# Attention's probabilities times values as two fp32r products with both parts of the values, and the stream's weights split in place

## The chip, the cores and the metric

The kernel runs on one core of one Trainium2 chip. The metric is device time in microseconds. Before the change the median of three runs is 1666.35 us (1666.28 to 1668.36).

## The reference, cut to what matters

One layer of a hybrid encoder, in fp32, over 1024 prompt frames and 64 new frames. D is 1024, there are 8 heads of 64 in each of two branches.

```python
z = rmsnorm(x, g_mix) @ w_in + b_in          # q,k,v of both branches, forget logits, two gates
# branch A: sliding window of 128, 8 q heads, 2 kv heads, bias and a sink per head
ya = softmax_with_sink(qa @ ka.T * SCALE + bias) @ va
# branch B: 8 heads, causal, logit += c[t] - c[s], c = cumsum(log_sigmoid(f))
yb = softmax(qb @ kb.T * SCALE + c_t - c_s) @ vb   # prompt: 1024 keys; new frames: 2048 cached + 64
x  = x + (sigmoid(ga) * (ya @ w_oa) + sigmoid(gb) * (yb @ w_ob)) @ w_out
x  = x + swiglu(rmsnorm(x))                   # then a final rmsnorm
```

The change touches `@ va` and `@ vb` of the prompt (and `@ va` of the new frames in branch A), and the order in which the weights of `w_in` are loaded and split.

## The kernel before, in words

Matmuls that must keep fp32's precision are made of fp32r matmuls (one pass each). An operand x is split into x_hi, a rounded copy that ScalarE writes as fp32r, and x_lo = x - x_hi, which VectorE writes. A product is then hi*hi + hi*lo + lo*hi, three matmuls (`split_product`, lines 2233 to 2235).

**Stages.** First x is normalised and transposed into `h_hi`, `h_lo`. Then the projection with `w_in` runs in 34 blocks of 128 output columns (`BLOCKS`). A block has three pieces (`dense(p)`, 24 matmuls each of 384, 384 and 320 columns), one for each third of the tokens. Pieces 0 to 17 stand before the stream. The **stream** is 136 attention units (steps 0 to 135) with pieces 18 to 85 laid between them, one in every even step. Units 0 to 71 are sliding-window units: four pairs of heads (`pair_start(p)` = 18p), nine tiles of 128 queries, two heads each. Units 72 to 135 are branch B's prompt ("fox"): four pairs, eight tiles, two heads; tile t has t + 1 blocks of 128 keys. Behind the stream stand four **decode units** (136 to 139, kind "new") for the 64 new frames with 2048 cached keys, with the last pieces 86 to 101 between them. Then come the merge with `w_oa`, `w_ob` and `w_out`, and the feed-forward part, which the change leaves as it is.

**A step.** Every engine has a list of instructions of its own in program order, and semaphores between them. TensorE's step n is `turn(n)` (transposes of unit n's probabilities into PSUM banks 4 and 5, four blocks to a group; line 2308), `scores(n + 2)` (line 2291), the transposes of `turns_at[n]`, `dense(piece_at(n))` if n is even, and `outputs(n - 1)` (line 2331): for each block of keys one matmul with the transposed probabilities as weights and 64 columns of values moving, plain fp32. In odd steps `turns_at` holds ("ot", n - 2), the transpose of the finished output of two units (line 2343); it waits for `o_evac`, the normalisation of unit n - 2. In even steps it holds ("tok", ...), keys and values turned to token order.

ScalarE's step n is `exp(n + 1)` (lines 1081 and 1083), `evac(piece_at(n - 1))` (line 1070, and behind a block's third piece `split_hi` of the block two further, line 1038), the even groups of `empty_groups` (line 561: PSUM to `probT` in SBUF), then the high parts of what was turned and staged. VectorE's step n is the odd groups of `empty_groups`, `scores(n + 2)` (line 1531: bias added, maximum taken), the low parts, `split_lo` (line 1478: `w_lo` = `w_raw` - `w_hi`), and `normalise(n - 1)` (lines 1553, 1554, 1562: the row sum's reciprocal, then bank 6 scaled into `o_tok`). With `outputs(n)` TensorE waits for the groups of unit n (`emptied`), and for `o_evac` of unit n - 1.

**Weights.** `w_raw`, `w_hi` and `w_lo` have two slots each. SyncE's queue loads block n once the low part of block n - 2 is written (`load_chunk`, lines 574 to 579), so loads run far ahead of their use. In the decode units `load_block(32)` stands before the first unit and `load_block(33 + s)` at the end of SyncE's part for unit s; `load_cache(s + 2)`, which loads the next cached keys into `kc_raw`, stands before it and waits until TensorE has turned all of the previous ones. TensorE's part of decode unit s is turn, cache part 0, piece d = 87 + 4s, cache part 1, outputs, cache part 2, piece d + 1, cache part 3, piece d + 2, output turn ("ots", line 2361), scores of the next unit, piece d + 3. The output turn waits for everything turned earlier to be emptied (`misc_done`).

```python
load_new(s + 1); load_values(s + 1)        # SyncE, decode unit s, before
...
if s < 2:
    load_cache(s + 2)
if s < 3:
    load_block(33 + s)
```

## Time and profile before

| | |
|---|---|
| median of the runs | 1666.35 us |
| the profiled execution | 1668.92 us, span 1667.1 us |
| TensorE matmul busy | 1609.9 us, 97% |
| TensorE weight loads | 1510.1 us, 91% |
| VectorE busy | 1018.6 us, 61% |
| ScalarE busy | 665.8 us, 40% |
| chain that ended last | TensorE 89%, DMA 4%, VectorE 4% |
| granted clock, mean | 0.989 |

The profiled execution is one run of the program; what lies around its span (1.8 us) is start and end. Matmuls are pipelined: the duration of one (some 275 ns) is longer than the time from its start to the next one's start, and only the latter adds up. So lists of rows in order of time are read by their starts. The stream lies from about 126 to 619 us, the decode units from there to 744 us.

### The profile page before, as it was taken

How to read it: one execution, taken by the hardware profiler on the slowest of the kernel's cores; microseconds unless marked ns; L12 is line 12 of the kernel's file. 1: busy time of each engine (PE TensorE's matmuls, PEld its weight loads, DVE VectorE, ACT ScalarE, POOL GpSimd, SP SyncE). 2: the span in 40 equal slices, each digit the busy share in tenths (PEclk: the TensorE clock that was granted, in tenths of full speed). 3: DMA queues.
4: the chain of work that ended last, by engine and by line, in shares of the span. 5: the costliest groups of instructions: out<-in, count | busy, mean ns of one | idle time of the engine just before them, and what ended most of it. 6: DMA issues, size and time to landing. Idle time of an engine off the chain costs nothing.

```text
span 1667.1 us, 27671 instructions
## 1 busy us (share of the span) xinstructions
PE 1609.9 (97%) x10556; PEld 1510.1 (91%) x10556; DVE 1018.6 (61%) x2232; ACT 665.8 (40%) x1333; POOL 174.7 (10%) x312
## 2 busy tenths in 40 slices
PE   6999999999999998999999899999999999989997
PEld 5999999999999998987898799999999999878886
DVE  6546556555546454426366586776677777659865
ACT  5335445544445434334253462222222223424443
POOL 3011111000000001012011000000122222110000
PEclk8999999999999999999999999999999999999999
DMA  6044331553351425648555323332344445766532
GB/s 205 26 127 131 121 107 66 181 163 95 116 146 47 120 91 166 193 148 283 187 158 198 120 76 104 98 97 78 100 154 154 154 154 180 245 188 188 152 121 94
DMA packets 190290, 230.59 MB, mean 138 GB/s; under 512 B 14807, under 2 KB 140280, under 8 KB 189640
## 3 DMA queue, kind: packets, MB, share of 16 engines
q1 hardware_dynamic: 163616, 138.71, 28.4%
q0 software_dynamic: 26544, 90.12, 15.3%
q8 instruction: 85, 1.39, 0.4%
q14 instruction: 45, 0.37, 0.1%
HBM read 166.76 MB, written 62.08 MB: 137 GB/s over the span
## 4 chain that ended last, share of the span: by engine, by line
PE 89%; DMA 4%; DVE 4%; issue 2%; ACT 1%; SPq 0%; POOL 0%; DVEq 0%; POOLq 0%
PE ps L2233 23%; PE ps L2235 23%; PE ps L2234 23%; PE ps L2331 6%; PE ps L2291 4%; PE ps L2308 3%; PE ps L2343 1%; PE ps L2511 1%; PE ps L2510 1%; DMA w_raw<-in_w_ob_dram 1%; DMA w_raw<-in_w_out_dram 1%; DMA xa<-in_x_prompt_dram 1%; PE ps L2254 1%; ACT w_hi L1038 1%; PE ps L2350 0%
## 5 line engine op out<-in xcount | busy, mean ns | idle before, releaser
L2233 PE MATMUL ps<-h_hi,w_hi 128*128 128x384 f32 (+1 forms) x816 | 275.1, 337 | 1.8 <-DVE w_lo L1478 1.1
L2235 PE MATMUL ps<-h_hi,w_lo 128*128 128x384 f32 (+1 forms) x816 | 268.2, 329 | 0.0
L2234 PE MATMUL ps<-h_lo,w_hi 128*128 128x384 f32 (+1 forms) x816 | 268.2, 329 | 0.0
L2235 PE MATMUL ps<-t_hi,e_lo 128*128 128x272 f32 x704 | 203.5, 289 | 0.0
L2234 PE MATMUL ps<-t_lo,e_hi 128*128 128x272 f32 x704 | 202.9, 288 | 0.0
L2233 PE MATMUL ps<-t_hi,e_hi 128*128 128x272 f32 x704 | 201.5, 286 | 0.9 <-DVE silu L1898 0.9
L2233 PE MATMUL ps<-b_hi,e_hi 128*128 128x272 f32 x528 | 152.4, 289 | 6.4 <-ACT p L1355 5.1
L2233 PEld LDWEIGHTS ps<-h_hi,w_hi 128*128 128x128 f32 x816 | 155.2, 190 | 3.2 <-DVE w_lo L1478 1.4
L2234 PEld LDWEIGHTS ps<-h_lo,w_hi 128*128 128x128 f32 x816 | 155.2, 190 | 0.5 <-issue 0.5
L2235 PEld LDWEIGHTS ps<-h_hi,w_lo 128*128 128x128 f32 x816 | 154.8, 190 | 0.0
L1562 DVE TENSOR_SCALAR o_tok<-ps,rinv 128x64 f32<-128x64 f32 x136 | 38.6, 283 | 188.9 <-PE ps L2331 186.7
L2235 PE MATMUL ps<-b_hi,e_lo 128*128 128x272 f32 x528 | 153.3, 290 | 0.0
L2234 PE MATMUL ps<-b_lo,e_hi 128*128 128x272 f32 x528 | 153.0, 290 | 0.0
L2233 PEld LDWEIGHTS ps<-t_hi,e_hi 128*128 128x128 f32 x704 | 132.8, 189 | 1.1 <-issue 1.1
L2235 PEld LDWEIGHTS ps<-t_hi,e_lo 128*128 128x128 f32 x704 | 132.4, 188 | 0.0
L2234 PEld LDWEIGHTS ps<-t_lo,e_hi 128*128 128x128 f32 x704 | 132.2, 188 | 0.0
L1070 ACT ACTIVATE stg<-ps,bin_cols 128x384 f32<-128x384 f32 (+1 forms) x96 | 53.8, 562 | 183.7 <-PE ps L2235 183.6
L2233 PE MATMUL ps<-e_hi,f_hi 128*128 128x512 f32 x308 | 120.9, 393 | 5.2 <-DVE e_lo L2116 5.2
L1083 ACT ACTIVATE sprob<-sprob,negm 128x256 f32<-128x256 f32 (+8 forms) x140 | 92.3, 659 | 77.0 <-DVE negm L1537 76.5
L2235 PE MATMUL ps<-e_hi,f_lo 128*128 128x512 f32 x308 | 120.8, 392 | 0.0
L2234 PE MATMUL ps<-e_lo,f_hi 128*128 128x512 f32 x308 | 120.8, 392 | 0.0
L1478 DVE TENSOR_TENSOR w_lo<-w_raw,w_hi 128x1024 fp32r<-128x1024 f32 x66 | 80.6, 1221 | 65.0 <-ACT w_hi L1038 64.7
(338 smaller groups left out, 3607.0 us busy)
## 6 DMA issues: line engine op xcount, KB each, us to landing
w_raw<-in_w_gu_dram SPq DMA_DIRECT2D x104, 256.0 KB, 3.3
w_raw<-in_w_in_dram SPq DMA_DIRECT2D x68, 256.0 KB, 3.2
zg_d<-stg POOLq DMA_DIRECT2D x28, 544.0 KB, 3.1
act_d<-act POOLq DMA_DIRECT2D x44, 272.0 KB, 2.7
s_d<-s_sum POOLq DMA_DIRECT2D x44, 256.0 KB, 3.3
f_raw<-s_d SPq DMA_DIRECT2D x44, 256.0 KB, 2.9
f_raw<-act_d SPq DMA_DIRECT2D x33, 256.0 KB, 3.0
w_raw<-in_w_out_dram SPq DMA_DIRECT2D x32, 256.0 KB, 3.4
```

The lines of the kernel that those rows point to most:

```text
L1038: nc.scalar.copy(w_hi[:, slot, :], w_raw[:, slot, :]).then_inc(w_hi_done, 1)
L1070: nc.scalar.activation(out, ps[:, bank_of(p), 0:c1 - c0], ACT.Identity, bias=bin_cols[:, col:col + 1]) \
L1083: nc.scalar.activation(probs, probs, ACT.Exp, bias=negm[0:R, c], accum_out=rowsum[0:R, c]).then_inc(p_ready, 1)
L1478: nc.vector.tensor_tensor(w_lo[:, slot, :], w_raw[:, slot, :], w_hi[:, slot, :].bitcast(F32), ALU.subtract) \
L1562: ins = nc.vector.tensor_scalar(o_tok[0:R, tl, HD * e:HD * e + HD], ps[0:R, 6, 0:HD], rinv[0:R, c], None, ALU.mult)
L2233: nc.tensor.matmul(out, l_hi, r_hi, start=start, stop=False)
L2234: nc.tensor.matmul(out, l_hi, r_lo, start=False, stop=False)
L2235: return nc.tensor.matmul(out, l_lo, r_hi, start=False, stop=stop)
L2254: last = nc.tensor.transpose(ps[:, norm_bank(tag, t, q), P * k:P * k + R], src[:, P * (4 * q + k):P * (4 * q + k) + P], ident[0:R, 0:R])
L2291: last = nc.tensor.matmul(ps[0:R, 2 + pc % 2, 0:w], lhsT, rhs, start=k == 0, stop=k == last_k and "diagonal" not in piece)
L2308: last = nc.tensor.transpose(ps[0:K, 4 + g % 2, (blk - b0) * R:(blk - b0) * R + R], score_room(u)[:, P * blk:P * blk + K], ident[0:R, 0:R])
L2331: last = nc.tensor.matmul(ps[0:R, 6, 0:w], probT[0:K, p0:p0 + R], val, start=blk == 0, stop=blk == nb - 1)
```

## The change

For stream units the transposed probabilities are split into `probT_hi` (in `probT`'s place) and `probT_lo` (in `w_lo`'s place), and the values into `va_parts` and `vb_parts`, which hold high and low parts side by side, 128 columns. For each block TensorE issues two fp32r matmuls of 128 columns, one with `probT_hi` and one with `probT_lo` as weights. Bank 6 then holds two halves whose sum is the output; `normalise` scales one and adds the other scaled. ScalarE writes the high part of every group, VectorE the low part. The decode units keep the fp32 product.

As `w_lo` is taken, blocks 6 to 29 (`IN_PLACE`) write their low part over `w_raw` (`w_rest`). A slot is then free only when TensorE has done its block, so the loads wait for `z_pe`. Splits of blocks 8 to 31 move: in the stream to four steps behind the last piece of block n - 2, in the decode units to the places below. Several tiles of the attention get other addresses, with the waits that follow from them.

```diff
+IN_PLACE = range(6, 30)
...
             def load_chunk(n, slot, parts):
-                if not isinstance(n, int) or n >= 2:
+                if n - 2 in IN_PLACE:
+                    sp.wait_ge(z_pe, 3 * (n - 1))
+                    hold()
+                elif n >= 2:
                     sp.wait_ge(w_lo_done, n - 1)
...
+            def load_pair_values(p):
+                if p > 4:
+                    sp.wait_ge(sem("s_k_lo"), value_count["b", p - 1, 1])
+                sp.dma_start(vb_tok[:, :, :, :], pv_fox[:, :, P * (p - 4):P * (p - 4) + P].rearrange("q t (e c) -> q t e c", e=2)) \
+                    .then_inc(sem("v_landed"), 16)
...
-                if step >= 1 and piece_at(step - 2) is not None and piece_at(step - 2) % 3 == 2:
-                    load_block(piece_at(step - 2) // 3 + 4)
+                d = piece_at(step - 1) if step else None
+                if d is not None and d % 3 == 2:
+                    load_block(d // 3 + 2)
...
-            load_block(32)
+            load_block(30)
             for s in range(4):
                 if s < 3:
                     load_new(s + 1)
...
                 if s < 2:
                     load_cache(s + 2)
-                if s < 3:
-                    load_block(33 + s)
+                if s == 0:
+                    load_block(31)
+                elif s < 3:
+                    load_block(30 + 2 * s)
+                    load_block(31 + 2 * s)
...
             pool.wait_ge(o_ready, N_UNITS)
-            pool.dma_start(gffn_row[:, :], g_ffn.broadcast_to([P, D])).then_inc(sem("gffn_landed"), 16)
             for j in range(5, KD):
                 load_gates(0, j)
             for slot in range(2):
                 pool.wait_ge(sem(f"abs_saved{slot}"), 64 * 2)
+            pool.dma_start(gffn_row[:, :], g_ffn.broadcast_to([P, D])).then_inc(sem("gffn_landed"), 16)
...
-                if s == 2:
+                if s == 2 and not 8 <= n + 2 < 32:
                     split_hi(n + 2, n % 2)
+
+            def values_hi(what):
...
+                if kind == "b":
+                    a.wait_ge(sem("v_landed"), 16 * (n - 3))
+                    a.wait_ge(o_ready, pair_start(n))
...
+                nc.scalar.copy(hi, raw).then_inc(sem("s_k_hi"), 1)
+
+            def turned_groups_hi(n):
+
+                u = units[n]
+                if n >= 2:
+                    a.wait_ge(o_ready, n - 1)
+                for g in range(u["group0"], u["group1"]):
+                    a.wait_ge(pt_ready, g + 1)
+                    for rows, cols, src in group_views(u, g):
+                        ins = nc.scalar.copy(probT_hi[rows, cols], src)
+                    ins.then_inc(sem("pt_act"), 1)
...
-                empty_groups(a, nc.scalar.copy, 0, units[n])
+                for what in values_at.get(n, ()):
+                    values_hi(what)
+                turned_groups_hi(n)
...
+            def turned_groups_lo(n):
+
+                u = units[n]
+                for g in range(u["group0"], u["group1"]):
+                    v.wait_ge(sem("pt_act"), g + 1)
+                    for rows, cols, src in group_views(u, g):
+                        ins = nc.vector.tensor_tensor(probT_lo[rows, cols], src, probT_hi[rows, cols].bitcast(F32), ALU.subtract)
+                    ins.then_inc(sem("pt_dve"), 1)
...
-                    ins = nc.vector.tensor_scalar(o_tok[0:R, tl, HD * e:HD * e + HD], ps[0:R, 6, 0:HD], rinv[0:R, c], None,
-                                                  ALU.mult)
+                    out = o_tok[0:R, tl, HD * e:HD * e + HD]
+                    chained(nc.vector.tensor_scalar(out, ps[0:R, 6, HD:P], rinv[0:R, c], None, ALU.mult))
+                    ins = nc.vector.scalar_tensor_tensor(out=out, in0=ps[0:R, 6, 0:HD], scalar=rinv[0:R, c], in1=out, op0=ALU.mult,
+                                                         op1=ALU.add)
...
+                    if u["kind"] == "new":
+                        last = nc.tensor.matmul(ps[0:R, 6, 0:P], probT[0:K, p0:p0 + R], val, start=blk == 0, stop=blk == nb - 1)
+                    else:
+                        nc.tensor.matmul(ps[0:R, 6, 0:P], probT_hi[0:K, p0:p0 + R], val, start=blk == 0, stop=False)
+                        last = nc.tensor.matmul(ps[0:R, 6, 0:P], probT_lo[0:K, p0:p0 + R], val, start=False, stop=blk == nb - 1)
```

In the decode units ScalarE's `split_hi(30)` now stands behind the second evacuation of unit 0, before the last cache part, and `split_hi(31)` behind the first evacuation of unit 1; `split_hi(32)` stays where it was, behind the second evacuation of unit 1 (piece 92). VectorE's low parts follow them. `values_at` puts the values' splits at steps 34 and `pair_start(p)` + 1 and + 2; those of the first two pairs stand before step 0.

## Rows read from the trace of the kernel before

**Rows 1.** Busy time by stage: stretch, its length, then busy (xcount) per engine, clock, DMA
```profile
126.00:344.00 218.00, 215.37 (x1452) 204.77 (x1451) 128.43 (x528) 107.48 (x332) 28.06 (x45) 1.00 0.37 118
344.00:619.00 275.00, 274.08 (x1975) 267.71 (x1976) 147.07 (x513) 130.98 (x280) 14.53 (x27) 1.00 0.39 116
```

**Rows 2.** The instructions of line 2331: duration min/median/max, first and last start
```profile
L2331 PE MATMUL ps<-vb_tok,probT x576: 217/275/295, 356.2 to 619.1; 128*128 128x64 f32 x192
...
L2331 PE MATMUL ps<-va_tok,probT x272: 217/275/323, 126.1 to 355.2; 128*128 128x64 f32 x120, 128*64 128x64 f32 x8, 64*64 64x64 f32 x8
```

**Rows 3.** In order of time: start, duration, engine, line, count; six fp32 products
```profile
602.79 1.45 PE L2331 MATMUL ps<-vb_tok,probT 128*128 128x64 f32 x12
...
604.08 0.93 PE L2308 MATMUL ps<-ident,sprob 128*128 128x128 f32 x7
```

**Rows 4.** In order of time: fp32r matmuls of 128 columns in a row
```profile
437.13 0.22 PE L2291 MATMUL ps<-k_stack,q_hi 128*128 128x128 f32 x1
...
437.19 0.27 PE L2291 MATMUL ps<-k_stack,q_lo 128*128 128x128 f32 x1
...
437.30 0.28 PE L2295 MATMUL ps<-causal_r,ident_r 128*128 128x128 f32 x1
```

**Rows 5.** In order of time: an odd sliding-window step around the output turn
```profile
203.00 0.28 DVE L1562 TENSOR_SCALAR o_tok<-ps,rinv 128x64 f32<-128x64 f32 x1 [1.01 <-PE ps L2331]
...
203.40 0.14 PEld L2343 LDWEIGHTS ps<-ident,o_tok 128*128 128x128 f32 x1 [0.26 <-issue]
...
203.56 0.48 DVE L1531 CUSTOM_DVE_ANT_0 sprob<-ps,bias,sink_rows 128x256 f32<-128x256 f32 x1
...
204.53 0.16 DVE L1554 RECIPROCAL rinv<-rowsum 128x1 f32<-128x1 f32 x1
...
204.73 0.28 DVE L1562 TENSOR_SCALAR o_tok<-ps,rinv 128x64 f32<-128x64 f32 x1
204.87 0.18 ACT L1083 ACTIVATION_READ_ACCUMULATOR sprob<-sprob,negm 128x1 f32 x1
```

**Rows 6.** Waits of TensorE's weight loads, 126 to 620 us: total, times, longest
```profile
PEld ps L2343 <- issue: 8.5, 33, 0.3
```

**Rows 7.** Groups of instructions of VectorE and ScalarE, 126 to 619 us: busy, mean ns
```profile
L561 DVE COPY probT<-ps 128x256 f32<-128x256 f32 x40 | 17.0, 424 | 1.9 <-PE ps L2308 1.8 <-issue 0.2
...
L1586 DVE TENSOR_TENSOR ot_lo<-ps,ot_hi 128x128 fp32r<-128x128 f32 x63 | 18.0, 285 | 0.0
...
L1478 DVE TENSOR_TENSOR w_lo<-w_raw,w_hi 128x1024 fp32r<-128x1024 f32 x22 | 26.8, 1218 | 0.1
...
L561 ACT COPY probT<-ps 128x256 f32<-128x256 f32 x32 | 11.3, 352 | 0.0
...
L1038 ACT CAST w_hi<-w_raw 128x1024 fp32r<-128x1024 f32 x22 | 22.8, 1036 | 0.0
```

**Rows 8.** In order of time: TensorE's waits around decode unit 0
```profile
630.46 0.66 PE L2308 MATMUL ps<-ident,sprob 128*128 128x128 f32 x4 [1.22 <-ACT probT L561]
...
654.11 0.50 PE L2291 MATMUL ps<-ks,qs_hi 128*128 128x512 f32 x1 [1.58 <-DVE maxpart L1531]
```

**Rows 9.** In order of time: the last cache part of decode unit 1
```profile
677.91 0.37 SPq L646 DMA_DIRECT2D kc_raw<-in_cache_fox_k_dram  x1
...
678.84 1.18 ACT L1100 CAST ks<-ps 64x512 fp32r<-64x512 f32 x2
...
680.24 1.39 DVE L1511 TENSOR_TENSOR ks<-ps,ks 64x512 fp32r<-64x512 f32 x2
...
681.92 0.27 PE L2361 MATMUL ps<-ident,o_tok 128*64 128x128 f32 x1
```

**Rows 10.** DMA issues: count, KB each, us to landing; 677 to 690, then 600 to 745
```profile
kc_raw<-in_cache_fox_k_dram SPq DMA_DIRECT2D x1, 1024.0 KB, 7.5
...
w_raw<-in_w_in_dram SPq DMA_DIRECT2D x4, 256.0 KB, 4.0
```

**Rows 11.** Busy time and granted clock, columns as in rows 1
```profile
956.00:960.00 4.00, 2.45 (x11) 2.48 (x12) 2.50 (x4) 2.87 (x6) 0.00 (x0) 0.50 0.04 13
```

More of the change, by code:

```diff
@@ L465, in build_program @@
                     pieces[-1]["diagonal"] = (P * t % 512, P, causal_r[:, :])
-                    units.append(dict(kind="fox", pair=p, rows=P, v=[vb_tok[s][:, j, HD * e:HD * e + HD] for j in range(t + 1)],
+                    units.append(dict(kind="fox", pair=p, rows=P, v=[vb_parts[:, j, e, :] for j in range(t + 1)],
                                       e=e, t=t, first=LOWEST, pieces=pieces))
@@ L495, in emptied, with value_views @@
         def emptied(g):
-            return sem(("pt_act", "pt_dve")[g % 2]), g // 2 + 1
+            if g < stream_groups:
+                return sem("pt_dve"), g + 1
+            return sem(("pt_act", "pt_dve")[g % 2]), stream_groups + (g - stream_groups) // 2 + 1
+        values = [("a", kv, x) for kv in range(2) for x in range(2)] + [("b", p, x) for p in range(4, 8) for x in range(2)]
+        value_count = {what: 7 + k for k, what in enumerate(values)}
+        values_at = {34: [("a", 1, 0), ("a", 1, 1)]}
+        for p in range(4, 8):
+            for x in range(2):
+                values_at[pair_start(p) + 1 + x] = [("b", p, x)]
+        def value_views(what):
+            kind, n, x = what
+            if kind == "a":
+                rows, tiles = (slice(0, P), slice(0, NT)) if x == 0 else (slice(0, DEC), slice(NT, NT + 1))
+                parts = va_parts[n]
+                return va_tok[rows, tiles, HD * n:HD * n + HD], parts[rows, tiles, 0:HD], parts[rows, tiles, HD:P]
+            tiles = slice(0, 2) if x == 0 else slice(2, NPT)
+            return vb_tok[:, tiles, :, :], vb_parts[:, tiles, :, 0:HD], vb_parts[:, tiles, :, HD:P]
         turns_at = {step: [] for step in range(N_STREAM)}
@@ L1191, in _ @@
                     stage_hi(what)
+                d = piece_at(n - 4) if n >= 4 else None
+                if d is not None and d % 3 == 2:
+                    split_hi(d // 3 + 2, d // 3 % 2)
             exp(N_STREAM)
@@ L1197, in _ @@
                 d = 87 + 4 * s
-                empty_groups(a, nc.scalar.copy, 0, units[N_STREAM + s])
+                empty_new(a, nc.scalar.copy, 0, units[N_STREAM + s])
                 if s < 3:
@@ L1477, in split_lo, with values_lo @@
                 v.wait_ge(w_hi_done, n + 1)
-                nc.vector.tensor_tensor(w_lo[:, slot, :], w_raw[:, slot, :], w_hi[:, slot, :].bitcast(F32), ALU.subtract) \
+                rest = w_rest if n in IN_PLACE else w_lo
+                nc.vector.tensor_tensor(rest[:, slot, :], w_raw[:, slot, :], w_hi[:, slot, :].bitcast(F32), ALU.subtract) \
                     .then_inc(w_lo_done, 1)
+            def values_lo(what):
+                raw, hi, lo = value_views(what)
+                v.wait_ge(sem("s_k_hi"), value_count[what])
+                nc.vector.tensor_tensor(lo, raw, hi.bitcast(F32), ALU.subtract).then_inc(sem("s_k_lo"), 1)
+            def turned_groups_lo(n):
+                u = units[n]
+                for g in range(u["group0"], u["group1"]):
+                    v.wait_ge(sem("pt_act"), g + 1)
+                    for rows, cols, src in group_views(u, g):
+                        ins = nc.vector.tensor_tensor(probT_lo[rows, cols], src, probT_hi[rows, cols].bitcast(F32), ALU.subtract)
+                    ins.then_inc(sem("pt_dve"), 1)
             def norm_recip_a(R, t):
@@ L1716, in _ @@
             scores(1)
+            values_lo(("a", 0, 0))
+            values_lo(("a", 0, 1))
             for n in range(N_STREAM):
-                empty_groups(v, nc.vector.tensor_copy, 1, units[n])
+                turned_groups_lo(n)
+                for what in values_at.get(n, ()):
+                    values_lo(what)
                 if n + 2 < N_STREAM:
@@ L2330, in outputs @@
                     p0 = turned_at(u) + blk * R
-                    last = nc.tensor.matmul(ps[0:R, 6, 0:w], probT[0:K, p0:p0 + R], val, start=blk == 0, stop=blk == nb - 1)
+                    if u["kind"] == "new":
+                        last = nc.tensor.matmul(ps[0:R, 6, 0:P], probT[0:K, p0:p0 + R], val, start=blk == 0, stop=blk == nb - 1)
+                    else:
+                        nc.tensor.matmul(ps[0:R, 6, 0:P], probT_hi[0:K, p0:p0 + R], val, start=blk == 0, stop=False)
+                        last = nc.tensor.matmul(ps[0:R, 6, 0:P], probT_lo[0:K, p0:p0 + R], val, start=False, stop=blk == nb - 1)
                 last.then_inc(o_ready, 1)
```

151 lines of the change are left out of this document (89 added, 62 removed).

## The prediction

> **What bounds the kernel now.** I read the busy time by stage first, then the waits, then stretches in order of time. In the stream (126 to 619 us) TensorE is busy for 215.37 of 218 and 274.08 of 275 us at full granted clock, while VectorE has 128 and 147 us of work and ScalarE 107 and 131 [rows 1]. So a step of the stream ends when TensorE's own list of instructions ends. Two kinds of edit can move the time there: one that changes what TensorE issues, or one that makes it wait. After the stream, in the four decode units, waits on VectorE and ScalarE do reach TensorE [rows 8].
>
> **The products.** The 424 products of probabilities and values stand as 848 matmul records, 576 and 272 [rows 2]: an fp32 product runs as two matmuls, each with its own weight load. Twelve records, six products, take 604.08 - 602.79 = 1.29 us, so one product costs 0.215 us [rows 3]. The new form issues two fp32r matmuls of 128 columns, each with its own weight load: again 848 records. What one costs shows where fp32r products of 128 columns stand in a row: when its weights had been waiting, the next came 0.06 us later (437.13 to 437.19), and with a load to make 0.11 us later (437.19 to 437.30) [rows 4]. The new kernel changes weights at every matmul, so I take the 0.11: two cost 0.22, against 0.215. The 64 idle columns that the old form leaves are given away free of charge, but nothing is won, because the weight load already sets the pace. 424 x 0.005 = 2 us; records after a wide matmul are hidden, so I take **+1** (ends: -41, below, and +2).
>
> The Trainium skill, page "TensorE: Matmul & The Clock Gate", section "Weight-path perf modes", says that the fast weight load is on for 128 weights unless the input is FP32. If fp32r counted as "not FP32", the change would win. Its section on LDWEIGHTS prices an ordinary load at columns over 1.2 per ns, 107 ns for 128, an estimate that would make two products 0.21 us; the 0.11 us in rows 4 agrees with that slow load.
>
> **Emptying the transposed probabilities.** Before, ScalarE and VectorE empty alternate groups. Now ScalarE copies every group as high part (256 columns: 352 ns) and VectorE then subtracts every group; a subtraction of 128 columns takes 285 ns and a VectorE copy of 256 takes 424 [rows 7], so I price a subtraction like a copy. It is a chain now: high part, low part, VectorE's scores, exp, next high part, which ScalarE's order puts after that exp. Scores and exp run from 203.56 to 205.05, 1.5 us [rows 5]; with 0.05 for each handover a sliding-window step is 0.35 + 0.42 + 1.5 + 0.1 = 2.4 us, a pair of steps 4.8, plus about 0.6 for the evacuation of the dense piece: 5.4. TensorE's pair is 218 / 36 = 6.1 us [rows 1]. The dense piece in every second step covers the chain, so this costs **0** while the chain is shorter. VectorE's load rises by 36 x 0.42 + 72 x 0.32 = 38 us in the sliding-window stage, to about 170 of 230, and by about as much in the fox stage. For the steps where token copies, split queries and values add to one another's delay I take **+2** (ends 0 and 20).
>
> **The extra operation in the normalisation.** The two halves of the output must be added: a scale, a wait on itself, and a scaled add, 0.28 + 0.04 + 0.28 where 0.28 stood (0.04 lies between the reciprocal's end at 204.69 and 204.73) [rows 5], +0.32 us. Who waits: in odd steps TensorE turns the output pair (L2343) right after scoring, and needs that normalisation. It ends at 203.28 and the weight load of the turn goes at 203.40, after a gap of 0.26 us [rows 5]. The waits list 33 such gaps, 8.5 us [rows 6]: none of these has cover left. By the loops, four of them open the fox pairs, where the value split below hides them, and 29 lie in the sliding-window stage: 29 x 0.32 = **+9.3**. In the fox pairs wider scores cover it from the fourth tile on; some twelve steps have less cover than 0.32 and no gap so far, I take 0.15 each, **+1.8** (0 to 3.8). The last output of the stream has none: **+0.3**.
>
> **Values split in the stream.** At each fox pair's start outputs wait for the first two value tiles to be split. That waits until the previous pair's last output is done, then 0.35 on ScalarE, the high part of a 128-wide group (about 0.25), its low part 0.29, the values' low part 0.42, and 0.2 of handovers: 1.6 us. TensorE has 0.9 of other work and waiting. 4 x 0.75 = **+3.0** (0 to 6). The remaining tiles have three steps of cover; those of the sliding window are split in VectorE's idle time before step 0 and beside a dense piece.
>
> **Weights split in place.** The low part overwrites the raw weights, so block n can be loaded only when the dense pieces of block n-2 are done, on SyncE's queue; it has six steps, some 20 us, before its first piece, and its split is due four steps after the release. Loads take 4 to 7.5 us to land [rows 10]. load_pair and load_new stand before some blocks on SyncE, but their waits are met a step or more earlier. No cost in the stream.
>
> Behind the stream the order changes. In decode unit 0, block 30 is no longer split before the turned groups, so the 1.22 us wait goes [rows 8], and block 31's split no longer stands before the scores, so the 1.58 us goes [rows 8]. But block 30's split (1.0 on ScalarE, 1.2 on VectorE) [rows 7] now stands before the last cache part, for which TensorE's output turn waits, so I let 1.1 us come back. Sum **-1.7** (-2.8 to 0).
>
> In decode unit 1 the new order hurts. Block 32 is now loaded behind load_cache(3), which waits for TensorE's fourth cache turn, so it is issued after kc_raw at 677.91, at 678.3. ScalarE splits block 32 right after its second evacuation (which had cost it nothing, as the load had long landed) and stands in order: behind it are the high parts of the cache (678.84) and of the new keys. VectorE's low part (680.24 to 681.63) waits for them, and TensorE's output turn (681.92) and the scores behind it wait for all [rows 9]. kc_raw took 7.5 us to land, block loads of the decode stage 4.0 in the median [rows 10]; sharing the queue with kc_raw, I take 7.5. Then: landed 686.0; high part of the block 687.1; cache high 688.3; block low 688.35; cache low 689.75; output turn 0.3 later, 690.05. The dense piece before it ends at 681.9 and covers nothing beyond that. **+8.1** (4.5 with 4.0 us). This is also 8 us of silence for TensorE: from 956 to 960 us, where TensorE stood and then resumed (busy 2.45 of 4), the granted clock was 0.50, the lower of the two levels (1.2 GHz) [rows 11]; 2 us of work then take 4. **+2** (0 to 4). Blocks 34 and 35 come later too; 34 now goes where 35 went, a dense piece and the next unit's scores ahead of its split: 0.
>
> The gffn load moves down GpSimd's queue, ahead of the second token group's loads, whose product it precedes by a whole output projection: 0.
>
> **Sum.** 1 + 2 + 9.3 + 1.8 + 0.3 + 3.0 - 1.7 + 8.1 + 2 = 25.8 us. The profiled execution took 1668.92 (span 1667.1, 1.8 around it), which gives 1694.7; it is 2.6 above the median of the runs, 1666.35, so on the median the forecast is 1692.
>
> **Rivals.** (a) Fast loads, the faster side: the fp32r weight load does not set the pace and a product of 128 columns costs the 0.06 of rows 4. Then 424 x (0.215 - 0.12) = 41 us go on TensorE, and with all else as above the time is 1666 + 26 - 1 - 41 = 1650. Against it: the 0.11 of rows 4 is just this load. (It is the skill's fast-load rule above, read that way.) Chance 0.08. (b) The chain bounds: if handovers and queued extras make the chain of two sliding-window steps 6.8 us instead of 5.4, it passes TensorE's 6.1 + 0.3, and 0.4 x 36 pairs = 14 us, and as much again in the fox pairs, come on top: 1720. It decides from 1.0 us more per pair than I count. For it: VectorE's token copies and splits stand in the same queue. Against: VectorE stays below three quarters busy. Chance 0.13. (c) Less than I say: block 32 lands in 4 us and the clock stays up (-5.6), value waits are covered (-3.0), collisions don't occur (-2): 1681. Chance 0.15. (d) No change: the output gap and the wait in unit 1 both hidden, 1668; against it every one of the 33 gaps. Chance 0.04. The forecast, 1683 to 1705: 0.60.
>
> The likeliest is 1692; the range 1676 to 1712 takes in (c) and the near half of (b). About 0.2% is what a measurement of this kernel can tell from no change: faster 0.08, same 0.04, slower 0.88.
>
> **What would show it.** L2331's successor: spacing 0.11 with two fp32r records per product (0.06 would prove rival a). The gap before the output turn about 0.55 instead of 0.26. One wait of 7 to 8 us before TensorE's output turn in decode unit 1, with ScalarE waiting for w_raw's DMA, and a dip of the granted clock behind it; no 1.58 us wait in unit 0. If TensorE's busy share in the stream drops below 0.95 at many small waits on probT or negm, rival (b) holds. I am wrong altogether if the stream is shorter than 493 us.

## The result and the profile after

The kernel after takes 1691.8 us (median; 1691.5 to 1693.4), the kernel before 1667.2 in the runs beside it (1666.3 to 1668.4): ratio 1.0147, 95% interval 1.0132 to 1.0161, so 24.6 us slower. The profiled execution of after has a span of 1689.7 us, 22.6 more than before's.

Busy time by stage (stretch, length, then busy us and count of TensorE, its weight loads, VectorE, ScalarE and GpSimd, granted clock, DMA); the stream now ends at 636 us, so the second row is longer than that of [rows 1]:

```profile
126.00:344.00 218.00, 205.73 (x1378) 195.74 (x1377) 153.47 (x601) 113.92 (x351) 28.06 (x45) 1.00 0.35 111
344.00:640.00 296.00, 290.45 (x2046) 281.11 (x2046) 202.36 (x671) 157.88 (x355) 14.52 (x27) 0.99 0.36 108
640.00:767.00 127.00, 112.44 (x697) 102.83 (x697) 46.65 (x103) 42.47 (x72) 10.16 (x19) 0.95 0.56 169
```

In the same 218 us TensorE is busy 205.73 us where it was busy 215.37 [rows 1]. Its products still make 848 records in the stream; it waits. Where, the waits of its weight loads say (total, times, longest; first 126 to 344 us, then, in the second block, 344 to 640):

```profile
PEld ps L2462 <- issue: 17.2, 31, 0.9
PEld ps L2462 <- DVE o_tok L1668: 0.5, 1, 0.5
```

```profile
PEld ps L2462 <- issue: 6.0, 16, 0.6
PEld ps L2449 <- DVE probT_lo L1582: 1.9, 4, 0.6
```

L2462 is the turn of an output pair (L2343 before). `issue` is idle time for which this view names no releaser; for such a gap TensorE's matmul rows name the normalisation, as in the last line of the next list. In [rows 6] the turn had 33 gaps of 8.5 us in the whole stream, 0.26 each; the 31 gaps of the first block are 0.55 each, the size that the prediction gave as its sign. L2449 is the product with the high part of the probabilities; its four waits are the four fox pair starts. In order of time, the products and an odd sliding-window step of after:

```profile
196.74 0.22 PE L2449 MATMUL ps<-va_parts,probT_hi 128*128 128x128 f32 x1
196.80 0.28 PE L2450 MATMUL ps<-va_parts,probT_lo 128*128 128x128 f32 x1
196.91 0.27 PE L2449 MATMUL ps<-va_parts,probT_hi 128*128 128x128 f32 x1
197.02 0.28 PE L2450 MATMUL ps<-va_parts,probT_lo 128*128 128x128 f32 x1
197.13 0.41 PE L2423 MATMUL ps<-ident,sprob 128*128 128x128 f32 x2
...
197.41 0.28 DVE L1667 TENSOR_SCALAR o_tok<-ps,rinv 128x64 f32<-128x64 f32 x1 [1.95 <-PE ps L2450]
197.73 0.28 DVE L1668 SCALAR_TENSOR_TENSOR o_tok<-ps,rinv,o_tok 128x64 f32<-128x64 f32 x1
...
198.16 0.30 PE L2462 MATMUL ps<-ident,o_tok 128*128 128x128 f32 x1 [0.38 <-DVE o_tok L1668]
```

The records stand 0.06 us apart behind the wide dense matmul and 0.11 apart from then on, as forecast. The two operations of the normalisation follow each other 0.32 us apart, and the turn waits for the second.

The decode stage has the wait that was forecast in unit 1. First its loads on SyncE's queue, then ScalarE's wait for the second of them, VectorE behind it, TensorE's output turn (L2480) behind that, in order of time:

```profile
694.08 0.37 SPq L692 DMA_DIRECT2D kc_raw<-in_cache_fox_k_dram  x1
694.56 6.00 SPq L619 DMA_DIRECT2D w_raw<-in_w_in_dram  x4
...
703.10 1.04 ACT L1089 CAST w_hi<-w_raw 128x1024 fp32r<-128x1024 f32 x1 [8.93 <-DMA w_raw<-in_w_in_dram]
704.05 1.17 ACT L1177 CAST ks<-ps 64x512 fp32r<-64x512 f32 x2
...
705.43 1.39 DVE L1615 TENSOR_TENSOR ks<-ps,ks 64x512 fp32r<-64x512 f32 x2
...
706.88 0.13 PEld L2480 LDWEIGHTS ps<-ident,o_tok 128*64 128x64 f32 x1 [8.95 <-DVE ks L1615]
```

The same stretch by its granted clock (length, TensorE busy, clock, DMA share, GB/s), which goes to half, the lower of its two levels:

```profile
698.00:702.00 4.00, 0.25 (x2) 0.84 1.08 359
702.00:706.00 4.00, 0.00 (x0) 0.50 0.58 175
706.00:710.00 4.00, 2.77 (x7) 0.50 0.03 8
710.00:714.00 4.00, 3.99 (x19) 0.88 0.04 8
```

To see where time goes in several kernels I took from each trace the starts of TensorE's output turns. They divide the execution at the same instructions everywhere (us from the start of the span to the first of them, then between these starts: the sliding-window stage from its first output turn to its last, the fox stage from there to the last output turn of the stream, then decode units 0 to 3 each to its own turn, then the rest of the span):

| kernel | to first turn | sliding window | fox | unit 0 | unit 1 | unit 2 | unit 3 | rest |
|---|---|---|---|---|---|---|---|---|
| before | 131.7 | 224.2 | 272.2 | 22.2 | 31.7 | 30.3 | 31.4 | 923.5 |
| after | 130.0 | 235.9 | 280.2 | 21.2 | 39.6 | 31.7 | 31.2 | 919.9 |
| e1_w32_early | 131.9 | 236.1 | 281.8 | 21.2 | 30.8 | 30.3 | 29.8 | 921.7 |
| e2_one_scale | 128.8 | 231.6 | 276.1 | 21.2 | 39.4 | 32.5 | 31.7 | 921.3 |
| e3_before_two_scales | 129.2 | 234.2 | 278.4 | 23.7 | 31.7 | 30.3 | 29.8 | 921.8 |
| e4_low_twice | 129.8 | 247.3 | 306.0 | 21.2 | 40.0 | 31.5 | 31.1 | 920.7 |
| e5_64_columns | 131.7 | 230.8 | 276.9 | 21.2 | 39.6 | 32.1 | 31.6 | 921.0 |
| e6_high_only | 129.5 | 227.9 | 253.6 | 21.2 | 39.5 | 31.8 | 31.3 | 921.1 |
| e7_before_new_order | 131.2 | 224.2 | 272.1 | 21.6 | 30.2 | 30.3 | 30.9 | 922.3 |
| e8_turn_low_first | 129.3 | 222.2 | 276.1 | 21.2 | 39.7 | 31.7 | 31.4 | 920.9 |
| e9_both_orders | 131.9 | 223.1 | 272.1 | 21.6 | 30.2 | 30.3 | 31.1 | 922.9 |
| e10_change_reordered | 130.2 | 234.0 | 279.0 | 21.2 | 30.8 | 30.3 | 31.4 | 920.3 |

The table settles where: 11.7 us in the sliding-window stage, 8.0 in the fox stage, 8.0 in unit 1 and 1.3 behind it, less 1.7 ahead of the stream, 1.0 in unit 0, 0.2 in unit 3 and 3.6 behind the decode stage. To the rounding that is the 22.6 us between the two spans.

### The profile page after: what moved, and what is told of

It reads as the page before. It is cut to its first block, busy times and chain, and to the rows that moved or that the text cites. A ratio compares the mean times of both kernels' runs of the same rounds, so it can differ in the third digit from the quotient of the medians.

```text
span 1689.7 us, 27986 instructions
## 1 busy us (share of the span) xinstructions
PE 1616.1 (96%) x10556; PEld 1513.5 (90%) x10556; DVE 1100.1 (65%) x2468; ACT 701.0 (41%) x1433; POOL 174.6 (10%) x312
## 4 chain that ended last, share of the span: by engine, by line
PE 89%; DVE 5%; DMA 2%; issue 2%; ACT 1%; SPq 1%; POOL 0%; DVEq 0%; ACTq 0%; POOLq 0%
PE ps L2348 24%; PE ps L2350 24%; PE ps L2349 24%; PE ps L2406 4%; PE ps L2450 3%; PE ps L2449 3%; PE ps L2423 3%; PE ps L2447 1%; PE ps L2462 1%; DVE o_tok L1667 1%; PE ps L2630 1%; PE ps L2629 1%; DVE o_tok L1668 1%; DMA xa<-in_x_prompt_dram 1%; PE ps L2469 1%
## 5 line engine op out<-in xcount | busy, mean ns | idle before, releaser
L2350 PE MATMUL ps<-h_hi,w_rest 128*128 128x384 f32 (+1 forms) x576 | 187.8, 326 | 0.0
L1667 DVE TENSOR_SCALAR o_tok<-ps,rinv 128x64 f32<-128x64 f32 x136 | 38.6, 284 | 119.2 <-PE ps L2450 116.7
L1423 ACT CAST e_hi<-w_sum 128x512 fp32r<-128x512 f32 x88 | 54.1, 616 | 134.3 <-DVE w_sum L1982 105.9
L2350 PEld LDWEIGHTS ps<-h_hi,w_rest 128*128 128x128 f32 x576 | 108.1, 188 | 0.0
```

The lines of the kernel that those rows point to most:

```text
L1423: nc.scalar.copy(e_hi[:, q % RING, :], src).then_inc(sem("e_hi_done"), 1)
L1667: chained(nc.vector.tensor_scalar(out, ps[0:R, 6, HD:P], rinv[0:R, c], None, ALU.mult))
L2350: return nc.tensor.matmul(out, l_lo, r_hi, start=False, stop=stop)
```

## The experiments

**The late load.** e1_w32_early:

```
-                elif s < 3:
-                    load_block(30 + 2 * s)
-                    load_block(31 + 2 * s)
+                    load_block(32)
+                elif s == 1:
+                    load_block(33)
+                elif s == 2:
+                    load_block(34)
+                    load_block(35)
```

> The kernel after, with one load moved on SyncE's queue: block 32 is issued in decode unit 0, behind block 31, in place of unit 1 behind the third cache part. My theory: the long wait before TensorE's output turn in unit 1 (9.0 us on VectorE's ks in the trace of after, with ScalarE 8.9 us on w_raw's DMA) comes from that load alone, and so does the granted clock of 0.50 behind it; both go: 8.8 + 1.1 = 10 us less than after, about 1682 (1680 to 1684). Rival: the order of the splits on ScalarE and VectorE in unit 1 is what costs, and the wait only changes its name: 1690 to 1692, with a wait of several us on another instruction in the same place.

It took 1684.1 us, ratio 1.0111 (1.0092 to 1.0131), that is 18.7 over before in the runs beside it (1665.3; the kernels of this section ran on several chips, so each is compared with before on its own). In its trace the four decode units take 112.2 us, 11.6 less than after (123.7): 8.8 in unit 1 and 1.3 and 1.4 in the two behind it. The 1.4 in unit 3 are not the load's. There the granted clock is 0.58 from 752 to 756 us in after, 0.57 from 726 to 730 us in before, and 1.00 throughout in e1 and in e3 below, which has the old loads; e10 below has e1's loads, shows 0.65 there and takes 31.4 us for the unit again. The load is worth 8.8 + 1.3 = 10.1 us. The loads go ahead of unit 1, and ScalarE splits the block with no wait behind its evacuation:

```profile
670.72 2.20 SPq L619 DMA_DIRECT2D w_raw<-in_w_in_dram  x4
...
688.79 0.58 ACT L1124 ACTIVATE stg<-ps,bin_cols 128x384 f32<-128x384 f32 x1 [3.02 <-PE ps L2353]
689.27 1.03 ACT L1092 CAST w_hi<-w_raw 128x1024 fp32r<-128x1024 f32 x1
```

The clock stays up (columns as above):

```profile
702.00:706.00 4.00, 3.62 (x15) 1.00 1.07 356
```

So the load alone makes that wait; the rival falls. The whole execution gained only 5.9 us against before, since outside the decode units this profile was 5.5 us longer than after's with the same instructions: at the start (a stretch at clock 0.57, 108 to 112 us, where after had 1.00), at the end of the stream (0.66 and 0.50 from 636 to 644 us, where after had 0.59 and 1.00) and in the rest. Its four runs spread from 1680.5 to 1686.2.

**The second operation, taken from after and put into before.** e2_one_scale (in after) and e3_before_two_scales (in before):

```
-                    chained(nc.vector.tensor_scalar(out, ps[0:R, 6, HD:P], rinv[0:R, c], None, ALU.mult))
-                    ins = nc.vector.scalar_tensor_tensor(out=out, in0=ps[0:R, 6, 0:HD], scalar=rinv[0:R, c], in1=out, op0=ALU.mult,
-                                                         op1=ALU.add)
+                    ins = nc.vector.tensor_scalar(out, ps[0:R, 6, 0:HD], rinv[0:R, c], None, ALU.mult)
```

```
-                    ins = nc.vector.tensor_scalar(o_tok[0:R, tl, HD * e:HD * e + HD], ps[0:R, 6, 0:HD], rinv[0:R, c], None,
-                                                  ALU.mult)
+                    out = o_tok[0:R, tl, HD * e:HD * e + HD]
+                    chained(nc.vector.tensor_scalar(out, ps[0:R, 6, 0:HD], rinv[0:R, c], None, ALU.mult))
+                    ins = nc.vector.scalar_tensor_tensor(out=out, in0=ps[0:R, 6, 0:HD], scalar=rinv[0:R, c], in1=out, op0=ALU.mult,
+                                                         op1=ALU.max)
```

> The kernel after with the old single operation in the normalisation: it scales the first 64 columns of the product only, so the low parts of the values are left out of the result; the products themselves, the splits and the loads stay. My theory: the second operation and its wait on itself lie on TensorE's path in the 29 odd steps of the sliding-window stage without cover (29 x 0.38 = 11), in some of the fox steps (1.8) and at the last output (0.3): 13 us less than after, 1679 (1676 to 1681). Rival: what lengthened the steps is the chain high part, low part, scores, exp; then the operation gives back 3 us at most, 1689 or more.

> The kernel before with a second, dependent operation in the normalisation and nothing else: a scale, a wait on itself, then a scaled maximum with the result (which leaves every value as it was). My theory: the same +13 us as in the other direction (11 to 16), so 1680 against 1667. Rival: in the old kernel the gaps before the output turn were made by something other than the end of the normalisation and there is cover: +4 at most, 1671.

e3 took 1681.2, ratio 1.0090 (1.0071 to 1.0108), 15.8 us more than before: 10.0 in the sliding-window stage, 6.2 in the fox stage. e2 took 1684.0, ratio 1.0112 (1.0096 to 1.0129), only some 6 us less than after, counted from before on each chip, where I had said 13. By stage it gives back 4.3 and 4.1, while its decode units take 1.0 longer. Put in, the operation costs 10.0 us in the sliding-window stage; taken out, it gives 4.3 back, and 7.4 us remain that are not its. That spoke for something like the rival. The waits of TensorE's weight loads from 126 to 344 us show what (L2460 in e2 is the output turn, L2467 and L2469 are the turns of a token block, which use the same room, bank 7; in e3, the first block, the output turn is L2345):

```profile
PEld ps L2345 <- issue: 17.7, 32, 0.7
```

```profile
PEld ps L2460 <- issue: 7.0, 29, 0.3
PEld ps L2467 <- DVE ot_lo L1690: 5.7, 14, 0.5
PEld ps L2469 <- DVE ot_lo L1690: 3.5, 8, 0.6
```

With one operation the gaps ahead of the output turn are back at their old size (29 of 7.0 us; before has 30 of 7.7 in this stretch), and 22 waits of 9.2 us are new: the token turn waits until VectorE has made the low part of the output turn (ot_lo). Both kernels in the same step, before first, then e2:

```profile
209.47 0.28 DVE L1562 TENSOR_SCALAR o_tok<-ps,rinv 128x64 f32<-128x64 f32 x1 [3.40 <-PE ps L2331]
209.69 0.42 DVE L561 COPY probT<-ps 128x256 f32<-128x256 f32 x1
210.03 0.48 DVE L1531 CUSTOM_DVE_ANT_0 sprob<-ps,bias,sink_rows 128x256 f32<-128x256 f32 x1
...
210.62 0.28 DVE L1586 TENSOR_TENSOR ot_lo<-ps,ot_hi 128x128 fp32r<-128x128 f32 x1
```

```profile
210.64 0.28 DVE L1667 TENSOR_SCALAR o_tok<-ps,rinv 128x64 f32<-128x64 f32 x1 [1.52 <-PE ps L2448]
211.27 0.42 DVE L1582 TENSOR_TENSOR probT_lo<-ps,probT_hi 128x256 fp32r<-128x256 f32 x1 [0.35 <-ACT probT_hi L1149]
211.61 0.48 DVE L1635 CUSTOM_DVE_ANT_0 sprob<-ps,bias,sink_rows 128x256 f32<-128x256 f32 x1
...
212.20 0.28 DVE L1690 TENSOR_TENSOR ot_lo<-ps,ot_hi 128x128 fp32r<-128x128 f32 x1
```

In before VectorE copied the turned group itself, 0.22 us after the start of its scale. Now it must wait for ScalarE's high part. That starts at 210.87, 0.23 us after the start of the scale, about where the copy stood: the evacuation ahead of it on ScalarE (0.58 us) has just ended. It takes 0.37 us, and only then the low part can begin. So the low part starts 0.63 us after the start of the scale, 0.41 later than the copy did, and everything behind it on VectorE, scores and ot_lo, shifts by as much. The kernel after, in the same step, has this too, but there VectorE fills its 0.35 us of waiting with the second operation, and the low part again starts 0.63 us after the start of the scale:

```profile
211.52 0.28 DVE L1667 TENSOR_SCALAR o_tok<-ps,rinv 128x64 f32<-128x64 f32 x1 [1.50 <-PE ps L2450]
211.84 0.28 DVE L1668 SCALAR_TENSOR_TENSOR o_tok<-ps,rinv,o_tok 128x64 f32<-128x64 f32 x1
212.15 0.42 DVE L1582 TENSOR_TENSOR probT_lo<-ps,probT_hi 128x256 fp32r<-128x256 f32 x1
...
213.08 0.28 DVE L1692 TENSOR_TENSOR ot_lo<-ps,ot_hi 128x128 fp32r<-128x128 f32 x1
```

So the two causes hide in each other. From one output turn to the next there are 24 pairs of steps with a token turn and, behind them, 11 without; against before they are longer, in sum (us, from the same starts as the table above):

| kernel | 24 pairs with token turn | 11 pairs without |
|---|---|---|
| e3_before_two_scales (second operation alone) | +6.5 | +3.5 |
| e2_one_scale (high and low parts alone) | +7.8 | -0.3 |
| after (both) | +8.1 | +3.6 |
| e8_turn_low_first (e2 without the path, below) | -1.6 | -0.4 |

One such pair, behind step 27, takes 6.16 us in before, 6.58 in e2 and 6.57 in after; one without, behind step 57, 5.67, 5.69 and 6.02.

**The path through ot_lo.** Taken out of e2's form by e8_turn_low_first:

```
+                early = [ev for ev in turns_at[n] if ev[0] == "ot"] if n < 70 else []
+                for ev in early:
+                    turned_lo(ev)
                 if n + 2 < N_STREAM:
                     scores(n + 2)
                 for ev in turns_at[n]:
-                    turned_lo(ev)
+                    if ev not in early:
+                        turned_lo(ev)
```

> e2_one_scale, with VectorE making the low part of the output turn ahead of its scores in the sliding-window stage, in place of behind them; nothing else. My theory: the 7.4 us that e2_one_scale still has over before in the sliding-window stage (231.6 against 224.2 from its first output turn to its last) are token turns that wait for this low part; the 22 waits on ot_lo (9.2 us) go and the stage is back at 224 to 226: 5.5 to 7.5 us less than e2_one_scale, 1677 to 1679. Rival: scores now come 0.3 us later and their exponentials and transposes with them, so the wait moves to TensorE's transposes of the probabilities: 1683 to 1685.

1675.2 us, ratio 1.0061 (1.0044 to 1.0078). The sliding-window stage takes 222.2 us, 9.4 less than e2's and 2.0 less than before's; no wait on ot_lo is left in it, and the output turn has its old gaps (the same view, same stretch):

```profile
PEld ps L2464 <- issue: 7.3, 30, 0.3
PEld ps L2464 <- DVE o_tok L1667: 0.2, 1, 0.2
```

The path is shown. It gave more than I expected of it, and the scores 0.3 us later cost nothing.

**Is the chain of high and low parts near the limit?** e4_low_twice:

```
+                        chained(nc.vector.tensor_tensor(probT_lo[rows, cols], src, probT_hi[rows, cols].bitcast(F32), ALU.subtract))
                         ins = nc.vector.tensor_tensor(probT_lo[rows, cols], src, probT_hi[rows, cols].bitcast(F32), ALU.subtract)
```

> The kernel after with the subtraction that makes the low part of the turned probabilities done twice, the second behind a wait on the first: the chain from high part to the output products is 0.33 to 0.73 us longer for each group, and VectorE has 72 x 0.46 = 33 us more to do in the sliding-window stage and about 64 x 0.8 = 51 in the fox pairs. My theory: TensorE's own list sets the time in the stream and the dense piece of every second step covers the chain, so it costs little: +0 to +3 in the sliding-window stage, +0 to +8 in the fox pairs (VectorE would be at 0.86 of that stage), 1692 to 1703. Rival (the chain of ScalarE and VectorE bounds the steps): half of the 84 us or more comes through, 1734 or above.

1730.4 us, ratio 1.0394 (1.0378 to 1.0411). That is 38.6 more than after's 1691.8, and 40.4 more when each is counted from before on its own chip. My theory of that moment failed: nearly half of the added 84 us comes through, as the rival said. In the sliding-window stage it is 11.4 us: 10.9 in the 24 pairs with a token turn, where 24 x 0.46 (0.42 and the wait on itself) would make 11.0, and 0.5 in the 11 without. That fits the ot_lo path again, not a limit of the chain as such. In the fox pairs it is 25.8 us, where TensorE's weight loads now wait for VectorE in many steps (344 to 640 us):

```profile
PEld ps L2407 <- DVE maxpart L1636: 6.2, 18, 0.5
PEld ps L2424 <- issue: 4.4, 7, 1.3
PEld ps L2424 <- DVE probT_lo L1583: 4.1, 9, 0.9
```

So in the fox pairs the low part was covered once, and not twice.

**What sets the pace of a product.** e5_64_columns makes both products of e2_one_scale 64 columns wide:

```
-                        nc.tensor.matmul(ps[0:R, 6, 0:P], probT_hi[0:K, p0:p0 + R], val, start=blk == 0, stop=False)
-                        last = nc.tensor.matmul(ps[0:R, 6, 0:P], probT_lo[0:K, p0:p0 + R], val, start=False, stop=blk == nb - 1)
+                        nc.tensor.matmul(ps[0:R, 6, 0:HD], probT_hi[0:K, p0:p0 + R], val[:, 0:HD], start=blk == 0, stop=False)
+                        last = nc.tensor.matmul(ps[0:R, 6, 0:HD], probT_lo[0:K, p0:p0 + R], val[:, 0:HD], start=False, stop=blk == nb - 1)
```

e6_high_only leaves the product with probT_lo out of after:

```
-                        nc.tensor.matmul(ps[0:R, 6, 0:P], probT_hi[0:K, p0:p0 + R], val, start=blk == 0, stop=False)
-                        last = nc.tensor.matmul(ps[0:R, 6, 0:P], probT_lo[0:K, p0:p0 + R], val, start=False, stop=blk == nb - 1)
+                        last = nc.tensor.matmul(ps[0:R, 6, 0:P], probT_hi[0:K, p0:p0 + R], val, start=blk == 0, stop=blk == nb - 1)
```

> e2_one_scale with both output products 64 columns wide in place of 128: the low parts of the values leave the products too (they were already left out of the result). My theory: the weight load of 0.11 us sets the pace of these products, whatever their columns, so the time is that of e2_one_scale, 1684 (1682 to 1686), and the records stand 0.11 us apart as before. Rival (the columns set the pace, 64 of them for each of 848 records, some 0.027 us each at the spacing of wide matmuls in the trace): up to 20 us less, 1664 to 1675.

> The kernel after without the product of the low parts of the probabilities (their subtraction on VectorE stays, its result is not used): 424 matmul records fewer, 144 in the sliding-window stage and 280 in the fox pairs, of 0.11 us each. Plain sum if TensorE's list alone set the time: 15.8 + 30.8 = 47 us less, 1645. My theory now, from e2_one_scale: in the 24 pairs of steps that have a token turn, that turn waits for the low part of the output turn, which VectorE makes behind the low part of the probabilities and its scores; that path does not get shorter, so these pairs give back nothing (at most 0.1 us each), and the sliding-window stage shrinks by 12 x 0.44 = 5 to 8 us of the 15.8; the fox pairs give most of their 31. Sum 34 to 39 less, 1653 to 1658.

e5 took 1686.4, ratio 1.0128 (1.0111 to 1.0144), against e2's 1.0112: the intervals overlap, and of the rival's up to 20 us nothing came. Its products, in order of time:

```profile
198.68 0.27 PE L2448 MATMUL ps<-va_parts,probT_lo 128*128 128x64 f32 x1
198.79 0.28 PE L2447 MATMUL ps<-va_parts,probT_hi 128*128 128x64 f32 x1
198.91 0.28 PE L2448 MATMUL ps<-va_parts,probT_lo 128*128 128x64 f32 x1
```

Half the columns, the same 0.11 us. The weight load sets the pace, and the rival of the columns falls. (The new kernel, too, has 0.06 us between two records only where the weights had been waiting behind a wide matmul.) e6 took 1658.7, ratio 0.9957 (0.9943 to 0.9972), 33 us less than after and not the 47 of the plain sum: 8.0 of 15.0 in the sliding-window stage and 26.6 of 31.7 in the fox stage. (The expectation counts 144 and 280 records; by the trace they are 136 and 288, at 0.11 us each.) The 24 pairs with token turns gave 4.3 of their 10.1, the 11 without 3.7 of 4.6. I had said 34 to 39; the fox stage gave 5 less than all. In it weight loads now wait for VectorE's maxima (2.6 us in 8 waits between 338 and 600 us), about half of that.

**Putting the orders right.** e10_change_reordered is the whole change with e1's loads, e8's order, and in VectorE's stream loop values_lo ahead of turned_groups_lo:

```
+                for what in values_at.get(n, ()):
+                    values_lo(what)
                 turned_groups_lo(n)
-                for what in values_at.get(n, ()):
-                    values_lo(what)
```

> The whole change with three orders mended: block 32's load early (e1_w32_early), the output turn's low part ahead of the scores in the sliding-window stage (e8_turn_low_first), and the values' low part ahead of the turned probabilities' low part on VectorE. My theory, by stage: decode units 112.2 us as in e1_w32_early in place of 123.7 (-11.5); the sliding-window stage is then left with the second operation of the normalisation alone, 232 to 234 in place of 235.9 (-2 to -4, less than the sum of both causes, since each hides in the other); the four pair starts -0.3 to -0.4 each (-1.5). Sum -15 to -17: 1675 to 1677 (a little more where the clock dips as it did in e1_w32_early), still 8 to 11 slower than before. Rival: the two causes in the sliding-window stage add up, and it goes to 228 or below.

1678.4 us, ratio 1.0072 (1.0055 to 1.0089), 11.5 over before, where I had said 8 to 11. The sliding-window stage is at 234.0, where e3, the old kernel with the second operation alone, is at 234.2: that operation is all that is left of the change there. The causes did not add up; taking the smaller one away gave 1.9 us, not 9.4. The four pair starts gave 0.4, 0.2, 0.3 and 0.3. The decode units take 113.7, 1.5 more than I said, and that is the clock in unit 3 (0.65 from 740 to 744 us), which e1 happened not to have.

**Is the new decode order of use without the products?** e7_before_new_order is before with the splits of blocks 30 and 31 on VectorE where after has them and e1's loads (the other splits are written out at their old places and are left out here):

```
-            load_block(32)
             for s in range(4):
...
-                if s < 3:
-                    load_block(33 + s)
+                if s < 2:
+                    load_block(32 + s)
+                elif s == 2:
+                    load_block(34)
+                    load_block(35)
...
-            split_lo(30, 0)
...
+                if s == 1:
+                    split_lo(31, 1)
...
+                if s == 0:
+                    split_lo(30, 0)
```

> The kernel before with the order of the decode stage that the new kernel has, and block 32's load ahead of the third cache part: block 30's low part goes from ahead of unit 0 to behind its second dense piece, block 31's from unit 0 into unit 1; loads 31 to 35 follow. Theory: the waits of 1.22 and 1.58 us in unit 0 go and 1.1 comes back, and without the late load nothing is lost in unit 1, as e1_w32_early showed (its four units took 112.2 us from the last turn of the stream to the last of the decode stage, before 115.6): 2 to 3.5 us less than before, ratio 0.998 to 0.999. Rival: with the old stream the block loads find something else late, and it is the same as before (1.000) or slower.

> e7_before_new_order, with the low part of the output turn ahead of VectorE's scores in the sliding-window stage, as in e8_turn_low_first: the old products with both better orders. Theory: e8_turn_low_first took 222.2 us from the first output turn of that stage to its last, where before took 224.2, so the order itself is worth 2 us in the old kernel too: 1661 on a chip where before takes 1666, ratio 0.997. Rival: those 2 us came from the new form (the high parts on ScalarE) and not from the order; then it is the same as e7_before_new_order, 0.998.

e7 took 1663.2 beside 1666.5 for before, ratio 0.9984 (0.9975 to 0.9993): 3.3 us less, as expected, and quicker than both kernels of this case. Its decode units take 113.1 us against 115.6, so 2.5 of it is where it should be. e9_both_orders adds e8's order of scores and ot_lo (its edit in before is the same): 1664.3 beside 1666.9, ratio 0.9980 (0.9970 to 0.9990), which is not to be told from e7, as the rival said. Its sliding-window stage was 223.1 us against 224.2 for e7, so 1.1 of the 2.0 us is there, too little for the medians to show. The other 0.9 does not come in the old form; no run shows why.

## Why the prediction was right, and where it was not

The forecast, 1692.0, lies 0.2 us from the median. The terms did not all hold as well as their sum, and that the sum comes so close is partly luck. By stage, from the two profiles: the stream was given 17.4 us (all terms but the decode units') and took 19.7; the decode units were given 8.4 and took 8.2; and 5.3 us came off ahead of the stream and behind the decode stage, where nothing was forecast. The spans differ by 22.6 us, not 25.8.

- **The products (+1).** Right: 0.11 us per record. In e8 the fox stage up to the last turn but one is 4.3 us longer than before's, and 2.9 of it are the pair starts; the 1.4 that remain are the 272 products between these turns at 0.005 us. Rival (a), the fast loads, is refuted: in e5 records of 64 columns with an fp32r load of 128 weights each stand the same 0.11 us apart. (Its price was 424 x 0.095 = 40, not 41.) The Trainium skill's rule ("TensorE: Matmul & The Clock Gate", "Weight-path perf modes") that loads are fast unless the input is FP32 does not hold here for fp32r.
- **The chain of high and low part (+2).** The step that failed. I compared the length of the whole chain with TensorE's pair of steps and found it covered. That was so for the probabilities themselves, but I did not ask who else stands behind the low part on VectorE. The low part of the output turn does, and the token turn needs bank 7 from it. By itself this costs 7.4 us in the sliding-window stage (e2 less before, and gone in e8). It is not rival (b) as I priced it, which was the scores' chain, with 14 us. Of that rival's sign, TensorE's busy share fell below 0.95 in the sliding-window stage (205.73 of 218 us, 0.94), but not over both rows of the stream (0.97), and the waits stood at the output turn.
- **The second operation (9.3 + 1.8 + 0.3).** Right in place and size for the sliding-window stage: alone it costs 10.0 (e3). The count was a little off: by the trace of before, 30 of the 33 gaps lie in that stage (30 x 0.32 = 9.6) and three, not four, open fox pairs. I took those as hidden by the value split, but the split delays the pair of steps behind: in after they cost 0.34 to 0.36 us each, in e2 0.02 to 0.04. In the fox stage e3 has 6.2 more, of which 3.3 us up to the last turn but one, where I said 1.8 (after has 6.7 there: 2.9 for the pair starts, 1.4 for the products, 2.4 for this). The last turn cost 2.9 in e3, 1.3 in after and 2.9 in e1, and the granted clock was down around it in all three (0.62 and 0.53, 0.59, 0.66 and 0.50 in stretches of 4 us; 1.00 in before), so most of this term is the clock's, where I had 0.3. It may still belong to the change: every kernel with the second operation shows such a stretch there, and of the six without it only e5. With one profile of each this is not shown.
- **Why the sum held.** This is the other piece of luck. The stage rose by 11.7 us, near 9.3 + 2, because the two causes overlap: 10.0 and 7.4 make 11.7 together and not 17.4. Had I found the second cause and put its 7.4 in place of the 2, the forecast for this stage would have been 5 us too high.
- **Values at the pair starts (+3.0).** Pair starts are 0.68 to 0.82 us longer, 2.9 together; the wait stood where I put it (four waits on probT_lo and four on vb_parts). Right, though the parts that I listed add up to 1.5 us and not 1.6, which would have made it 2.4.
- **Weights split in place (0 in the stream).** No wait of an engine in after or e8 from 126 to 640 us names w_rest or w_raw, and e8, which has all of it, runs the sliding-window stage in 222.2 us.
- **Decode unit 0 (-1.7)**: -1.0 up to its turn and about -0.8 behind it. The wait of 1.58 us is gone.
- **Unit 1 (+8.1) and the clock (+2).** The load was issued at 694.56 and landed 8.5 us later (I took 7.5); the wait cost 8.8 and the clock 1.3 more in the next unit (after less e1). 10.1 predicted, 10.1 measured.
- **Not predicted.** After is 1.7 us shorter ahead of the first turn, where before had a stretch at clock 0.57 (108 to 112 us) and after did not; kernels of both kinds show it either way, so it is no effect of the change. The stretch behind the decode stage is 3.6 us shorter. 1.3 us of it is a wait of TensorE for w_lo that before has near 773 us (1.6 us, by its weight loads) and after has not. The other order of the loads is not shown to be the cause: e3, with the old order, waits 0.5 us there at most, and e9, with the new order, 2.1 us. Another 1.2 us lies where the granted clock was down for longer in before (0.86, 0.50 and 0.78 from 952 to 964 us) than in after (0.58 from 980 to 984 us only). The rest is in two smaller places. The stretch takes 921.8 and 923.5 us in the kernels with the old order (e3 and before) and 919.9 to 922.9 in those with the new one, and whether the order does anything there stays open.

## What to carry to other kernels

Before an operation is moved to another engine or made to wait for one, list everything that stands behind it in that engine's order, not only who uses its result: here one of the two causes came through an unrelated turn that shared a bank. Causes that sit in the same step are not to be added; put one into the old kernel and take it out of the new one, and where the two numbers differ (10.0 and 4.3 here) another cause is hidden beneath. And a load that is moved behind a wait on its queue can be paid with its whole landing time: here ScalarE met it in order, VectorE and TensorE stood behind ScalarE, and 8.8 us went. So look first at where each engine will meet the load.

## What the runs showed of the hardware

An fp32 product of 64 columns, which runs as two records, and two fp32r products of 128 columns take the same time to 0.005 us (0.215 and 0.22), and fp32r products of 64 columns are no quicker: with new weights each time the load of 0.11 us is the price. A dependent pair of VectorE operations on 128x64 elements is 0.32 us from start to start, 0.28 of it the first. The granted clock was down for some 4 us around 108 us in some profiles (0.57 in before and in e1) and not in others (1.00 in after and in e3), although e1 and after have the same instructions up to there; profiles with it reach the first output turn after 131.2 us or more, those without it after 130.2 or less. Around the last output turn of the stream it was down for about 4 us in after and about 8 in e1, again with the same instructions, and that made 1.5 us. A single profile shows such scatter as if it were a difference between kernels.
